# Products of zeros in the waits of the expert stages of a two-layer trunk

## What is computed

```python
g_prob = softmax(x @ w_rg + b_rg); p_group, g_idx = top_k(g_prob, 1)
e_in = expert logits of that group
top_p, top_i = top_k(softmax(e_in), 2)
gates = one_hot(g_idx * 8 + top_i) * (top_p / sum(top_p) * p_group)
hid = silu(einsum("nd,edf->nef", x, w_g)) * einsum("nd,edf->nef", x, w_u)
y = einsum("nef,efd->nd", hid * gates, w_d)
```

## Time and profile before

| | |
|---|---|
| time, median of 3 runs | 810.34 us (807.7 to 811.61) |
| span of the profiled execution | 809.0 us (the profile gives no other time of this execution) |
| TensorE busy | 741.6 us, 92% of the span, 6795 matmuls |
| VectorE, ScalarE, GpSimd busy | 309.2, 160.7, 13.5 us |
| moved by DMA | 291.46 MB, mean 360 GB/s |
| mean granted TensorE clock | 0.972 |

### The profile page before, as it was taken

The page is one execution under the profiler, slowest core; times in us unless marked ns, Lnnn a source line. Parts: engine busy times, 40 slices in busy tenths (PEclk is TensorE's granted clock), DMA queues, the critical chain, the costliest instruction groups (busy, mean ns, idle before and its releaser), DMA issues.

```text
span 809.0 us, 15683 instructions
## 1 busy us (share of the span) xinstructions
PE 741.6 (92%) x6795; PEld 495.1 (61%) x6795; DVE 309.2 (38%) x676; ACT 160.7 (20%) x315; POOL 13.5 (2%) x17
## 2 busy tenths in 40 slices
PE   3999999998899999999948799999999999994877
PEld 3787468677799656555534354799855555552425
DVE  1154577662513534344330240251543334433024
ACT  3112321323213211111110041130411111111103
POOL 0000001020100000000000000000000000000000
PEclk9999999999999999999988999999989999997898
DMA  9999889493899899999999999997679999999991
GB/s 341 386 373 382 323 303 351 133 343 105 276 409 414 325 425 418 415 420 421 421 422 414 398 386 385 388 410 313 213 293 422 419 417 420 421 421 420 414 389 63
DMA packets 90647, 291.46 MB, mean 360 GB/s; under 512 B 11769, under 2 KB 14927, under 8 KB 73167
## 3 DMA queue, kind: packets, MB, share of 16 engines
q1 hardware_dynamic: 79728, 284.32, 89.7%
q10 hardware_dynamic: 10847, 6.11, 2.6%
HBM read 288.30 MB, written 2.10 MB: 359 GB/s over the span
## 4 chain that ended last, share of the span: by engine, by line
PE 68%; SPq 17%; DMA 6%; DVE 3%; issue 2%; ACT 2%; ACTq 1%; DVEq 0%
PE psum L1289 7%; SPq L751 6%; PE psum L1382 6%; PE psum L1357 6%; PE psum L910 5%; PE psum L989 5%; PE psum L1367 5%; SPq L769 5%; PE psum L1416 4%; PE psum L863 4%; PE psum L1559 3%; PE psum L1577 3%; SPq L740 3%; PE psum L1427 3%; SPq L741 2%
## 5 line engine op out<-in xcount | busy, mean ns | idle before, releaser
L1367 PE MATMUL psum<-ring,hT 128*32 128x512 f32 (+1 forms) x304 | 75.0, 619 | 14.0 <-DMA scratch<-in_w_exp_up 14.0
L1367 PE MATMUL psum<-scratch,hT 128*32 128x512 f32 (+1 forms) x368 | 75.0, 624 | 12.7 <-DMA ring<-in_w_exp_up 12.7
L1357 PE MATMUL psum<-scratch 128*128 128x128 f32 x640 | 78.3, 282 | 2.1 <-DVE scratch L2510 2.1
L1357 PEld LDWEIGHTS psum<-scratch 128*128 128x128 f32 x640 | 75.9, 198 | 2.3 <-issue 2.2
L910 PE MATMUL psum<-hT,ring 128*128 128x256 f32 x256 | 57.8, 382 | 1.1 <-DVE hT L2098 0.6
L910 PEld LDWEIGHTS psum<-hT,ring 128*128 128x128 f32 x256 | 47.8, 190 | 9.6 <-DVE hT L2098 1.9
L1427 PEld LDWEIGHTS psum<-const,scratch 128*128 128x128 bf16 x432 | 40.5, 97 | 17.9 <-issue 12.9
L1427 PE MATMUL psum<-const,scratch 128*128 128x256 bf16 x432 | 50.4, 272 | 0.0
L2519 DVE TENSOR_SCALAR hT<-psum,const 128x512 f32<-128x512 f32 x20 | 15.0, 751 | 85.7 <-PE psum L1416 84.2
L1367 PEld LDWEIGHTS psum<-scratch,hT 128*32 128x32 f32 (+1 forms) x368 | 20.9, 118 | 43.5 <-issue 43.5
L1931 ACT ACTIVATE scratch<-psum 128x256 f32<-128x256 f32 x20 | 7.7, 384 | 199.8 <-PE psum L1367 127.7
(11 more groups left out here) (347 smaller groups left out, 988.4 us busy)
## 6 DMA issues: line engine op xcount, KB each, us to landing
ring<-in_w_mod SPq DMA_DIRECT2D x40, 1024.0 KB, 12.1
scratch<-in_w_exp_down SPq DMA_DIRECT2D x32, 1024.0 KB, 20.1
ring<-in_w_exp_down SPq DMA_DIRECT2D x24, 1024.0 KB, 19.1
scratch<-in_w_exp_gate SPq DMA_DIRECT2D x22, 1024.0 KB, 18.9
scratch<-in_w_exp_up SPq DMA_DIRECT2D x22, 1024.0 KB, 21.0
ring<-in_w_exp_gate SPq DMA_DIRECT2D x18, 1024.0 KB, 19.3
ring<-in_w_exp_up SPq DMA_DIRECT2D x18, 1024.0 KB, 21.3
scratch<-in_w_exp_gate SPq DMA_DIRECT2D x24, 512.0 KB, 12.3
```

The source lines that it names most:

```text
L1357: last = mm(bank[b][:, k * P:(k + 1) * P], hrow[:, t, half * 4 + k, :], Pm[:, t, :], start=(t == 0), stop=(t == 1))
L1367: last = mm(bank[0][i * m:(i + 1) * m, :], xg[:, k, i * m:(i + 1) * m], w[e][:, k, :, :], start=(k == 0), stop=(k == KT - 1))
```

## The change

Products of zeros are added at five places of TensorE's program and nowhere else: four after the position counts of `moe`; two ahead of `rows_of_tables` in pass 0; two ahead of `order_tables`; and in each of the passes 1 to 8 two ahead of the wait of the scatter and two ahead of the waits of `turn`. They go into banks 6 and 3, whose contents nothing needs at those points. No other instruction is removed or moved.

```diff
--- before.py
+++ after.py
@@ -1329,6 +1329,7 @@
                 for t in range(NB):
                     last = mm(bank[0][0:NE, 3 * NE:3 * NE + 1], msk[:, t, :], ones[:, 0:1], start=(t == 0), stop=(t == 1))
                 last.then_inc(S.t_pos, 1)
+                idle_products(6, 4)
 
             def rows_of_tables(l):
 
@@ -1383,6 +1384,7 @@
                                       w[i // 2][:, i % 2, k, :, :], start=(kh == 0 and k == 0), stop=(kh == 1 and k == 3))
                     last.then_inc(S.used, n)
                     if kh == 0 and tables is not None:
+                        idle_products(6, 2)
                         rows_of_tables(tables)
                     if kh == 0 and between is not None:
                         idle_products(3, 3)
@@ -1467,10 +1470,13 @@
                             mm(bank[4 + b], zeros[:, 0:1].to_broadcast([32, P]), zeros[:, 0:1].to_broadcast([32, 512]), start=True, stop=True, skip_group_check=True)
 
                     if 0 < q < NPASS - 1:
+                        idle_products(3, 2)
                         pe.wait_ge(S.m_yr1, n)
                         scatter()
                     if q == NPASS - 1:
                         idle_products(3, 3)
+                    if 0 < q < NPASS - 1:
+                        idle_products(3, 2)
                     pe.wait_ge(S.m_hid, n + 1)
                     pe.wait_ge(S.m_p, 2 * n + 2)
                     turn(S.m_turn)
```

## The result

The changed kernel took 822.13 us (median of 4 runs, 820.09 to 823.66), the kernel before 810.98 us (807.7 to 813.62, 4 runs): a ratio of 1.0125, 95% interval 1.0086 to 1.0163. The changed kernel is slower, by 11 us, where no change was forecast, and the time lies outside the range. The profiled execution took 823.66 us with a span of 821.8 us, 12.8 us more than that of the profiled execution before.

What follows compares the result with a forecast made beforehand. Each expert stage was taken as bound by a fixed 180 us weight stream, leaving TensorE spare time. 809.0 + 2 x 0.53 - 3.13 = 806.9 us profiled, carried over as 810.34 - 2.07 = 808.3 us; range 805.0 to 812.2.

Steps and rivals of the forecast that it cites:

- Part by part: Section pricing the added products at each of their places: 0.53 us per layer at the order tables, 0 elsewhere.
- the rivals: Four alternatives: no clock gain (0.22), more falls gone (0.18), fall moved to layer 0 (0.07), leak through the queue (0.08).
- I take 3.13: Layer 1's first gathers: the four products prevent the clock fall, gaining 3.13 us out of 0 to 3.13.
- rival A: Clock fall at the gathers not removed, or chance; only the pairs' cost remains: 811.4 us, chance 0.22.
- the prediction's first sign of being wrong: A clock fall at either layer's first gather would show the forecast wrong; no size given.
- a pair costs 0.53 us at the order tables: Two products ahead of `order_tables` push the second gather and first L1382 group: +0.53 us per layer, on the path.
- four products fit under the wait: After the position counts: four products take 0.97 us inside waits of 1.07 and 1.03 us, cost 0.
- the streams: Expert weight loads of each layer: first issue to pass 9's last half stays at 180 to 181 us.
- nothing leaks from the passes: Passes 1 to 8: 1.06 us more per pass is covered by waits for weights, cost 0.
- L1276 has 119 records: Sign of being right: the line of the added products shows 39 + 16 + 64 = 119 records.

Runs made afterwards that it cites:

- the control: The changed kernel run again with no edit, against the kernel before: 815.78 us over 12 runs, ratio 1.0049.
- the kernels without the jump: TensorE's branch in `moe_further` replaced by the arm taken here: changed kernel 811.75 us (1.0020), kernel before 810.10 us (0.9985).
- the three further ones: Three more executions of the changed kernel, no edit, each profiled: 819.23, 825.64 and 819.62 us.

## Why the prediction was wrong

**The step that failed first** is the one that isn't there. "Part by part" prices each product at its own place and takes the instructions behind it to run as before; no sentence asks what 160 more instructions do to the place of the code behind them; that term stands at nothing, without a reason. None of the rivals has it either. The profiled executions separate without exception: with a stall at the last jump 32.7 to 34.9 us pass from the last half to the end (8 executions, of the changed kernel and of kernels without its products), without one 25.6 to 28.0 us (10 executions). 1.8 to 2.7 us of the difference are the stall. Behind it the same products run at the low clock: the group of L1436 (by its line in the changed kernel) takes 3.0 to 3.8 us instead of 1.97, the second group of L1509 1.71 instead of 0.95 in seven of the eight. Displacing the code alone costs 1.4%, displacing it by a whole packet 0.1%, which is nothing within its interval, and putting the changed kernel back on the packet takes its ratio from 1.0049 in the control to 1.0006. Clearer still is the pair with the passes' products: 1.0050 (1.0032 to 1.0068), and 1.0006 (0.9988 to 1.0024) with 64 products more. That the cause is where the code behind the jump lies, and not the length of the program or the products, is shown by these runs, and by the kernels without the jump. That TensorE waits there for the fetch of that code is read from the packets, 2.4 to 2.9 us ahead of the next product.

The Trainium skill has the rule, which I didn't draw on (Runtime: NRT & Kernel Launch, Instruction fetch mechanics): code comes in blocks of 16 KiB, 256 instructions, read ahead in order only, and a taken branch to a block that isn't at hand has to fetch it. The packets of 16384 bytes agree with it, and so do the kernels displaced by 256 instructions, which behave like those displaced by none. It gives no time for the fetch; here TensorE stood 1.8 to 2.7 us at the last jump, and 2.38 and 5.26 us at layer 0's.

**The clock.** "I take 3.13" was the second failure, and rival A, without that gain, was the right one of those named. The four products don't keep the clock up, and the prediction's first sign of being wrong, a fall at either first gather, came at once. Of the profiled executions, nine have them: 12 of their 18 first gathers lost clock, 2.75 us in each execution (over 4.93 us per layer). Eight don't: 7 of 16, 1.70 us in each (over 4.40). These numbers are too few to say that the products bring falls, but they show no gain. Eight products in place of four did no better, in one profiled execution. The layer in which the fall comes changes from one execution to the next, also in kernels that are the same up to there. The trace of before showed one such draw, and I took it for a property of layer 1.

**Right, in mechanism and size:** a pair costs 0.53 us at the order tables (4.93 and 4.94 against 4.40), though no run shows that the 0.09 us over two steps are the array being handed back; four products fit under the wait (1.32 us from the counts to the gather in layer 1, as before) as long as the clock holds; where it fell under them, in layer 0 of two executions, the gather came 0.33 and 0.67 us later; the streams last 179.9 to 181.7 us in all profiled executions, whatever TensorE does beside them; nothing leaks from the passes that the runs can tell (their 64 products measured 1.0006, known to 2 us); L1276 has 119 records. By these steps alone the forecast is that of rival A, 810.34 + 1.06 = 811.4 us, and the changed kernel without a stall measured 811.75 and 811.88. That it comes so close is in part luck: the runs tell 2 us apart, and the falls at the gathers come on top.

**What of the 11 us is accounted for.** In the profiled execution 6.18 us are the end, 4.71 layer 0's gathers (0.53 of it the pair, the rest the longer fall), 1.69 the low clock in layer 0's last half, 1.79 lie ahead of the first change, and 2.59 are won at layer 1's gathers. Over many executions the picture is milder: the control gave 815.8 us, not 822.1. Two things stay open. The five executions of the control at 809.5 to 811.5 us look like executions without a stall: their mean granted clock is 0.984 to 0.989, that of the upper cluster 0.979 to 0.985. But none of them was profiled, the kernel without the jump reaches 816.77 us too, and nothing here says why the same code would stall in one execution and not in the next. And why the first four executions all lay at 820 us or more isn't settled; the three further ones, at 819 to 826 us and on another chip than the control, have the stall and a fall at the gathers of both layers.

None of these kernels is faster than the one before by half a per cent. The lowest ratio is that of the kernel before with 40 one-column products (0.9976); without TensorE's jump it is 0.9985, and that kernel can't do the work that the left-out arm is for.

## What to carry to other kernels

Instructions have a place as well as a duration. Where an engine's program has a taken branch, an edit anywhere ahead of it can bring a stall there that has nothing to do with what the edit does (here 1.8 to 2.7 us at the end, and as much as 1.4% of the time in all); try the edit once more with its instruction count filled up to a whole packet, or displace the old kernel by as much, before judging it. And a fall of the clock seen in one execution is one draw: look at the same place in other layers and executions before spending products on it.

## What the runs showed of the hardware

The clock can stay low with TensorE busy all the time: 10.2 us at 0.50 through four products of zeros, gathers of 128 columns and two more products, with no wait recorded from 268.7 us on, 2.6 us ahead of the fall. In that execution the low clock ended about where the up products of 512 columns began (281.5 us), but in the control's, between 274.4 and 274.6 us, still among the gathers. A stall of some 2.2 us at a jump cost two to three times as much in all (about 6.5 us at the end, 5.0 in layer 0), since the clock fell behind it; the one of 5.26 us cost about 7.5.
